# Order of TensorE's work inside a step of the attention heads of a two-layer decoder: transposes first, both halves of the projection unit last

## What is computed

```python
def diff_attention_block(q, k, v, q_pos, k_pos, lam, slopes):
    """q (B,Q,H,2,d) pre-scaled; k (B,K,H,2,d); v (B,K,H,2d). (softmax1 - lam*softmax2) V with ALiBi, causal."""
    s = jnp.einsum('bqhcd,bkhcd->bhcqk', q, k).astype(jnp.float32)
    dist = (q_pos[:, None] - k_pos[None, :]).astype(jnp.float32)
    s = s - slopes[None, :, None, None, None] * dist
    s = jnp.where(dist >= 0, s, -jnp.inf)
    p = jax.nn.softmax(s, axis=-1)
    w = p[:, :, 0] - lam * p[:, :, 1]
    return jnp.einsum('bhqk,bkhe->bqhe', w.astype(v.dtype), v)
...
proj = h @ w_in_odd[j]
q, k, v = jnp.split(proj, 3, axis=-1)
```

## Time and profile before

| | |
|---|---|
| three runs, median (lowest to highest) | 3040.63 us (3035.64 to 3041.06) |
| profiled execution, span | 3041.2 us |
| TensorE matmul busy | 2859.2 us, 94% |
| TensorE weight load busy | 2743.5 us, 90% |
| VectorE busy | 1539.2 us, 51% |
| ScalarE busy | 1033.3 us, 34% |
| GpSimd busy | 584.7 us, 19% |
| heads of layer 1, first value product to the last step of head 6 | 1703 to 2047 us |

### The profile page before, as it was taken

One profiled execution on the slowest core, in us unless ns is written; L12 is line 12 of the kernel. 1 busy time (PEld: TensorE's weight loads), 2 busy tenths in 40 slices (PEclk: granted clock), 3 DMA queues, 4 the chain that ended last, 5 costly groups with the idle time before them and its releaser, 6 DMA issues. The chain is left out here.

```text
span 3041.2 us, 46041 instructions
## 1 busy us (share of the span) xinstructions
PE 2859.2 (94%) x18498; PEld 2743.5 (90%) x18498; DVE 1539.2 (51%) x2304; ACT 1033.3 (34%) x1747; POOL 584.7 (19%) x321
## 2 busy tenths in 40 slices
PE   6999988979999999999989999995899999999997
PEld 5999978849899999999979888884889999999996
DVE  3057434346753444444482577774565444444436
ACT  3325534425511111111162466663562111111114
POOL 1212134400132222222100122210003222222220
PEclk8999989979999999999999999997899999999999
DMA  4111100033321111111141122223431111111103
GB/s 147 49 43 36 29 10 0 1 94 103 107 70 55 41 41 41 41 41 55 28 134 45 54 87 73 74 63 139 124 107 56 55 54 42 41 41 41 41 14 113
DMA packets 183498, 185.01 MB, mean 61 GB/s; under 512 B 10469, under 2 KB 168549, under 8 KB 183296
## 3 DMA queue, kind: packets, MB, share of 16 engines
q1 hardware_dynamic: 183380, 183.45, 19.5%
HBM read 151.13 MB, written 32.57 MB: 60 GB/s over the span
## 5 line engine op out<-in xcount | busy, mean ns | idle before, releaser
L1554 DVE TENSOR_TENSOR acc<-acc,ps 128x1032 f32<-128x1032 f32 x144 | 176.9, 1229 | 232.0 <-PE ps L124 232.0
L1958 PE MATMUL ps<-mix_in0hi,in0wh 128*128 128x344 f32 x600 | 197.6, 329 | 14.9 <-POOL mix_in0lo L244 9.1
L124 PE MATMUL ps<-midlo,rest0wh 128*128 128x344 f32 x984 | 209.1, 321 | 0.0
L124 PE MATMUL ps<-mix_out1lo,rest1wh 128*128 128x344 f32 x984 | 209.0, 321 | 0.0
L124 PE MATMUL ps<-midhi,rest0wl 128*128 128x344 f32 x984 | 208.6, 320 | 0.0
L124 PE MATMUL ps<-mix_out1hi,rest1wh 128*128 128x344 f32 x984 | 208.6, 320 | 0.0
L124 PE MATMUL ps<-midhi,rest0wh 128*128 128x344 f32 x984 | 208.5, 320 | 0.0
L124 PE MATMUL ps<-mix_out1hi,rest1wl 128*128 128x344 f32 x984 | 208.5, 320 | 0.0
L1958 PE MATMUL ps<-mix_in0lo,in0wh 128*128 128x344 f32 x600 | 192.8, 321 | 0.0
L1958 PE MATMUL ps<-mix_in0hi,in0wl 128*128 128x344 f32 x600 | 192.8, 321 | 0.0
L124 PEld LDWEIGHTS ps<-midhi,rest0wl 128*128 128x128 f32 x984 | 165.6, 188 | 0.0
(11 more groups left out here) (508 smaller groups left out, 6990.0 us busy)
## 6 DMA issues: line engine op xcount, KB each, us to landing
wraw<-in_w_ffn_gate SPq DMA_DIRECT2D x22, 1024.0 KB, 5.4
wraw<-in_w_ffn_up SPq DMA_DIRECT2D x22, 1024.0 KB, 5.3
wraw<-in_w_ffn_down SPq DMA_DIRECT2D x22, 1024.0 KB
wraw<-x_scratch SPq DMA_DIRECT2D x96, 172.0 KB, 3.2
x_scratch<-acc SPq DMA_DIRECT2D x72, 172.0 KB, 3.2
wraw<-in_w_in_even SPq DMA_DIRECT2D x24, 512.0 KB, 3.9
wraw<-in_w_in_odd SPq DMA_DIRECT2D x24, 512.0 KB, 4.5
sr_page<-in_cache_k SPq DMA_DIRECT2D x16, 512.0 KB, 4.1
```

What stands on the lines that cost most here:

```text
L124: ins = pe.matmul(ps[:, 3 * r + c, 0:CH], w, h[:, c * CH:(c + 1) * CH], start=first and n == 0, stop=last and n == 2)
L1554: dve.tensor_tensor(a, a, region(T.ps, m % 2), ALU.add).then_inc(collected, 1)
L1958: ins = pe.matmul(bank(n, c), w[n % 2][:, k, :], cut(h[:, k, :], c), start=first and m == 0, stop=final and m == 2)
```

## The change

Only TensorE's `step` and `head` are rewritten. A step keeps all its operations and their waits, and their order is new: scores of tile i+3 (steps 0 to 4), value product, the turns of k, v or output (they stood behind the step before), the transposes of tile i+1, the scores of 0' to 2' (steps 5 to 7), and then the halves of the projection unit, both together where a step has two. Before, the first half stood between the value product and the transposes of tile i+1, and the second one at the end of the step.

```diff
--- before.py
+++ after.py
@@ -2992,30 +2992,32 @@
                         ins = pe.matmul(av, wt[:, i % 2, t, :], vt[:, t, :], start=t == 0, stop=t == i)
                     ins.then_inc(av_made, 1)
 
-                def step(h, p, i, more):
+                def other_turns(h, p, i, more, first):
+                    if i == 1:
+                        turn_kv(h, 3)
+                    if i in (2, 3) and not first:
+                        turn_output(h - 1, 1 - p, i - 2, 4 * h + 4)
+                    if i >= 5 and more:
+                        turn_kv(h + 1, i - 5)
+
+                def step(h, p, i, more, first):
                     here, coming = ahead(h, p, i, 1, more), ahead(h, p, i, LEAD, more)
                     if coming is not None and coming[2] >= LEAD:
                         score(coming[0], coming[2])
                     if i >= 0:
                         times_values(h, i)
-                        if more:
-                            unit(h + 1, HALVES[i][0])
+                        other_turns(h, p, i, more, first)
                     if here is not None:
                         turn_weights(here[0], here[2])
                     if coming is not None and coming[2] < LEAD:
                         score(coming[0], coming[2])
+                    if i >= 0 and more:
+                        for half in HALVES[i]:
+                            unit(h + 1, half)
 
                 def head(h, p, more, more2, first):
                     for i in range(NQ):
-                        step(h, p, i, more)
-                        if i == 1:
-                            turn_kv(h, 3)
-                        if i in (2, 3) and not first:
-                            turn_output(h - 1, 1 - p, i - 2, 4 * h + 4)
-                        if i >= 5 and more:
-                            turn_kv(h + 1, i - 5)
-                        if more and len(HALVES[i]) > 1:
-                            unit(h + 1, HALVES[i][1])
+                        step(h, p, i, more, first)
                     if not more:
                         for n in range(2):
                             turn_output(h, p, n, 4 * H)
@@ -3036,7 +3038,7 @@
                     turn_kv(0, 2)
                     pe.wait_ge(qs_moved, 2)
                     for i in range(-LEAD, 0):
-                        step(0, 0, i, True)
+                        step(0, 0, i, True, True)
 
                 run_heads(pe, start, head)
```

## The result

The changed kernel takes 3056.89 us (median of 4 runs, 3054.08 to 3060.95) against 3040.85 us for the kernel before, measured beside it: ratio 1.0054, 95% interval 1.0042 to 1.0067. It is slower by 16 us, 0.5%. The forecast had it slower by 10, with 3057 as the upper end of its range; the median lies on that end, and the measured loss is 1.6 times the forecast one.

The account below looks back on a forecast made before the run. TensorE was taken to set the pace in the seven heads with a projection, busy 333.6 of 347 us. Terms 10.2 - 3.5 - 2.1 - 1.5 + 6.8 = +9.9 us on 3041.2 gave 3050 us, range 3036 to 3057.

Parts of the forecast that it names:

- (1): Transposes of tile 6, steps 4 and 5: without half 8 ahead they wait 2.8 us for VectorE; +10.2 us over seven heads.
- (5): Behind the new wait at tile 6 the clock falls in 4.5 of 7 heads: +6.8 us, bounds 0 and 10.5.
- (4): Between the loop's passes: ScalarE reaches its branch earlier, TensorE waits less, -2.1 us, and the clock holds, -1.5 us.
- (3): Seams between TensorE's operations, turns and starts of halves: cheaper in the new order, -3.5 us over seven heads.
- VectorE's chain: Steps 4 and 5, value product of tile 4 to mix of tile 6: held by GpSimd, ends as before, 0.
- head 7: Makes no projection; turns of the output change place with transposes that wait for VectorE anyway: 0, bounds -1 and +1.
- rival B: Clock falls in every head, 3054 us, or GpSimd also collides with step 7's mix of tile 0', 3060 us; chance 0.13.
- One sign of being wrong: Steps 4 and 5: forecast wrong if the mix of tile 6 ends earlier than 9.4 us behind the product of tile 4.
- Part (2): Transposes of tile 5, step 4: wait about 0.2 us for the value product's bank, hidden under tile 6's wait: 0.
- Rival C: Step 4: GpSimd's multiply misses VectorE's two-column operation, tile 6 could be turned 2.1 us earlier: 3029 us; chance 0.10.

Follow-up runs that it names:

- run 3: Changed kernel with 12 filler matmuls more per head in step 5, between the value product of tile 5 and the turn of k: 3046.30 us, ratio 1.0019.
- run 2: Kernel before with the new order in step 5 alone (turn of k ahead of tile 6's transposes, half 8 behind them): 3064.22 us, ratio 1.0079.
- run 6: Changed kernel with half 8 put back in step 5 and ScalarE's high parts of the second weight slot made a step later: 3030.63 us, ratio 0.9968.
- run 1: Changed kernel with half 8 put back in step 5, between the value product of tile 5 and the transposes of tile 6: 3035.53 us, ratio 0.9981.
- run 5: Kernel before with the new order in step 7 alone (turn of v ahead of the transposes of 0', half 11 last): 3036.66 us, ratio 0.9988.
- run 4: Changed kernel with GpSimd's multiply of each head's second cache page cut from 1024 to 64 columns, leaving work out: 3030.89 us, ratio 0.9965.
- run 8: Changed kernel with VectorE's reduction of the first cache page moved from the end of its step 3 to step 2: 3031.22 us, ratio 0.9969.
- run 10: Kernel before with VectorE's reduction of the first cache page moved from the end of its step 3 to step 2: 3035.27 us, ratio 0.9981.

## Why the forecast was right in its direction and short in its size

The chain of reasons held: the wait for the bank vanished, a wait of 2.4 to 3.0 us for VectorE took its place at the transposes of tile 6 in all seven heads, VectorE's chain kept its length within 0.4 us, GpSimd's multiply was what held it, and the loop gave time back. The terms, for heads 0 to 6:

| term of the sum | forecast | measured | from |
|---|---|---|---|
| (1) matmuls without cover, step 5 | +10.2 | +10.4 | run 3, 7 x (5.28 - 3.79) |
| (5) clock behind the wait | +6.8 | +13.4 | 23.8 in the seven stretches, less 10.4 |
| (4) between the loop's passes | -3.6 | -4.9 | 1916.59 - 1910.74 against 10.77 before |
| (3) seams | -3.5 | -2.1 | steps 1, 3, 6, 7, and 0 without heads 0 and 4 |
| not in the sum: step 2 | 0 | +3.1 | 5.6 to 5.7 us, before 5.0, in five heads |
| not in the sum: step 0 of head 0 | 0 | +1.9 | 8.23 against 6.36, the clock |
| VectorE's chain | 0 | -1.9 | from product 4 to transposes 6, 72.9 us, before 74.8 |
| sum | +9.9 | +19.9 | 367.5 against 347.6 |
| head 7 | 0 | -3.4 | 44.3, before 47.7 |

**The step that failed is part (5).** The mechanism was named and one fall priced at 1.5 us, but I counted 4.5 falls of seven from three waits elsewhere in the program. All seven fell. The price was right for five of them (6.79 - 5.28 = 1.5 us), and two lasted twice as long: for head 1 the stretch was 8.24 us, which is 3 us of clock. Forecast +6.8, measured +13.4; its own upper bound of 10.5 was too low. Why none of the seven held, and why it was heads 1 and 5 that fell for longer, here and in run 2, stays open. The filler of run 3 shows this term by itself: the wait shorter, the work more, and 10.6 us back.

**Missing from the sum was the second collision,** step 2. The forecast asked whether GpSimd might win over VectorE in step 7 (rival B), and didn't ask it in steps 1 and 2, where the transposes and the turn of v moved ahead of the projection just as well. It costs 3.1 us, and run 6 takes it away. Run 6 is 5 us faster than run 1, on another chip; in their traces step 2 accounts for 3.1 of it.

**Head 7** I put at 0 with bounds of 1. By the two traces it gave 3.4 us, but against the 45.5 us of the same order in runs 2 and 5 only 1.2, and runs 3 and 6 with the new order took 45.3 and 45.7. So the record doesn't show that it gave anything, and 0 may have been right.

**One sign of being wrong came true.** The forecast named itself wrong if the mix of tile 6 ended earlier than 9.4 us behind the product of tile 4. It ended 1840.55 - 1831.58 = 9.0 behind it. The lock let go as far behind the chain's start as before (5.2 us, before 5.1), but it held a later operation, so 0.4 us less of the chain was left behind it. The sign was set too tight for what it was to tell.

Part (2) was right to be there and to be hidden. Part (4) was right in its place, shown by run 5, and too small by 1.3 us: it left a wait of 1.5 us, and none was there. Part (3) was too large by 1.4. Rival C, faster because VectorE isn't held, was 0.10 by chance and 3029 us by its working: it didn't happen by itself, but runs 4 and 8 made it happen, at 3031. That the forecast came within 7 us of the median owes something to luck: for heads 0 to 6 it was 10 us short, its errors in (3) and (4) cancelled, and some 4 us came back outside these heads.

## What to carry to other kernels

Ahead of moving filler work, find the tightest chain that it covers and write down its slack: here six steps of eight were free to reorder, a seventh cost 3 us, and one half in the eighth had nothing to spare, as the transposes behind it already waited 0.2 us, and cost 24. Count a new idle gap of 2.4 us or more of TensorE at its own length plus a fall of the clock each time it comes, not at a share: 13 of the 14 such gaps in step 5 (changed kernel and run 2) brought one. And when an engine is released earlier, follow it to GpSimd. Ask too what binds a chain next: taking away GpSimd's hold brought the transposes of tile 6 forward by 0.1 us in the old order, where ScalarE held as long, and by 1.4 to 1.7 us in the new one.

The new order with one reduction moved is 0.3% faster than the kernel before (run 8), with half 8 left in place 0.2% (run 1). But the old order with the same reduction moved is 0.2% faster too (run 10), and the intervals of runs 8 and 10 overlap: that the new order itself is worth anything beside that is not shown.

## What the hardware showed that I had not expected

- Behind waits of TensorE of 2.43 to 3.01 us the granted clock went to 0.50 in seven heads of seven in the changed kernel, in two of them for some 7 us. In run 2 it held once behind 2.88 us and fell behind the other six, of 2.88 to 3.22. Behind the waits of up to 1.34 us at tile 6 in runs 1, 3, 4 and 8 it held every time.
- An operation on one column took 2.17 us beside a GpSimd multiply that the profile starts 0.24 us ahead of it (1834.54 and 1834.78), and before the change one on two columns took 2.44 us though the profile starts it 0.03 us ahead of the multiply. The Trainium skill (SBUF — State Buffer, Who interferes with whom) has the one that issues first take the ports. The starts that the profile shows are too close in the second case to tell which was first, so it neither bears that out nor contradicts it.
- Eight operations of VectorE on 128 columns, 2.19 us together, became 4.33 us when one GpSimd instruction of 2.40 us started among them: 2.14 us are added, once.
